# Direction 1 of the doubling levels moved to the array's off-diagonal quadrants, and the output norm's root moved from ScalarE to GpSimd

## The reference, cut to what matters

```python
def step(S, inp):
    r_t, w_t, kk_t, a_t, k_t, v_t = inp
    sa = jnp.einsum('bhvk,bhk->bhv', S, -kk_t)
    S = S * w_t[:, :, None, :] + sa[..., None] * (kk_t * a_t)[:, :, None, :] + v_t[..., None] * k_t[:, :, None, :]
    return S, jnp.einsum('bhvk,bhk->bhv', S, r_t)
...
o = outs[0] + outs[1]
mu = jnp.mean(o, -1, keepdims=True)
var = jnp.mean(jnp.square(o - mu), -1, keepdims=True)
o = ((o - mu) * lax.rsqrt(var + RWKV_GN_EPS)).reshape(B, T, BRANCH_WIDTH) * p['rwkv_gn_g'] + p['rwkv_gn_b']
```

## Time and profile before

| | |
|---|---|
| median of 3 runs | 2651.05 us (2650.5 to 2652.39) |
| the profiled execution | 2649.7 us, its span 2645.4 us |
| PE busy, share of the span | 2505.4 us, 95% |
| DVE busy, share of the span | 1384.3 us, 52% |
| the four passages of layer 2, from the first gram matrices to the tail | about 2041 to 2236 us |
| the same of layer 1 | about 741 to 936 us |

### The profile page before, as it was taken

One profiled execution on the slowest core, in us unless ns is written; L12 is line 12 of the kernel. 1 busy time (PEld: TensorE's weight loads), 2 busy tenths in 40 slices (PEclk: granted clock), 3 DMA queues, 4 the chain that ended last, 5 costly groups with the idle time before them and its releaser, 6 DMA issues.

```text
span 2645.4 us, 56785 instructions
## 1 busy us (share of the span) xinstructions
PE 2505.4 (95%) x23398; PEld 2338.5 (88%) x23398; DVE 1384.3 (52%) x2306; ACT 1053.0 (40%) x1709; POOL 329.2 (12%) x316
## 2 busy tenths in 40 slices
PE   5999999999989999999979999999999999899998
PEld 3888989889988888999968899998898889899997
DVE  2333355576587655443353334646766775644434
ACT  3333244355633434332253332434555342343323
POOL 0000032000033304000100001210001332220001
PEclk7999999999999998999989999999999999989999
DMA  8766634332300023446466665333232000334373
GB/s 271 245 221 191 192 92 135 88 90 81 104 3 4 28 62 97 127 128 203 119 210 220 222 193 157 106 110 86 87 89 72 4 4 27 103 99 126 114 222 108
DMA packets 482186, 319.95 MB, mean 121 GB/s; under 512 B 15474, under 2 KB 438920, under 8 KB 481800
## 3 DMA queue, kind: packets, MB, share of 16 engines
q1 hardware_dynamic: 481928, 316.32, 39.1%
HBM read 311.30 MB, written 4.98 MB: 120 GB/s over the span
## 4 chain that ended last, share of the span: by engine, by line
PE 43%; DVE 4%; issue 1%; ACT 1%; POOL 1%; DMA 0%; SPq 0%; DVEq 0%; ACTq 0%; POOLq 0%
PE acc L849 11%; PE acc L851 10%; PE acc L850 10%; PE pb L1204 3%; PE acc L1204 2%; PE pb L903 1%; PE pb L911 1%; PE pb L918 0%; PE pb L1132 0%; POOL ln_sum L2033 0%; DVE xt L2533 0%; PE pb L1151 0%; PE pb L849 0%; DVE w_lo L2147 0%; PE pb L1119 0%
## 5 line engine op out<-in xcount | busy, mean ns | idle before, releaser
L849 PE MATMUL acc<-xm_hi,w_hi 128*128 128x384 f32 x2352 | 810.5, 345 | 37.3 <-DVE xm_lo L2157 33.1
L851 PE MATMUL acc<-xm_hi,w_lo 128*128 128x384 f32 x2352 | 795.3, 338 | 0.0
L2147 DVE TENSOR_TENSOR w_lo<-raw,w_hi 128x1024 fp32r<-128x1024 f32 (+1 forms) x420 | 521.4, 1241 | 510.8 <-ACT w_hi L1581 502.6
L850 PE MATMUL acc<-xm_lo,w_hi 128*128 128x384 f32 x2320 | 784.3, 338 | 0.0
L1581 ACT ACTIVATE w_hi<-raw 128x1024 fp32r<-128x1024 f32 (+1 forms) x420 | 438.8, 1045 | 284.9 <-PE acc L851 180.1
L849 PEld LDWEIGHTS acc<-xm_hi,w_hi 128*128 128x128 f32 x2352 | 448.6, 191 | 80.1 <-issue 50.8
L851 PEld LDWEIGHTS acc<-xm_hi,w_lo 128*128 128x128 f32 x2352 | 447.8, 190 | 0.0
L850 PEld LDWEIGHTS acc<-xm_lo,w_hi 128*128 128x128 f32 x2320 | 442.3, 191 | 0.5
L849 PE MATMUL acc<-h_hi,w_hi 128*128 128x384 f32 x704 | 242.6, 345 | 8.2 <-DVE w_lo L2147 8.1
L851 PE MATMUL acc<-h_hi,w_lo 128*128 128x384 f32 x704 | 239.9, 341 | 0.0
L850 PE MATMUL acc<-h_lo,w_hi 128*128 128x384 f32 x704 | 239.6, 340 | 0.0
(11 more groups left out here) (364 smaller groups left out, 3476.3 us busy)
## 6 DMA issues: line engine op xcount, KB each, us to landing
raw<-in_ffn_w_in SPq DMA_DIRECT2D x179, 512.0 KB, 4.0
modw<-in_w_mod SPq DMA_DIRECT2D x71, 1024.0 KB, 6.1
raw<-in_w_in SPq DMA_DIRECT2D x114, 512.0 KB, 4.0
raw<-in_ffn_w_out SPq DMA_DIRECT2D x64, 512.0 KB, 4.9
raw<-in_ffn_w_out SPq DMA_DIRECT2D x32, 384.0 KB, 3.6
raw<-in_w_up SPq DMA_DIRECT2D x24, 512.0 KB, 3.5
modx<-in_w_mod SPq DMA_DIRECT2D x9, 1024.0 KB, 12.8
raw<-in_w_out SPq DMA_DIRECT2D x16, 512.0 KB, 4.4
```

The costliest lines, as they stand in the source:

```text
L849: pe.matmul(out, lhs[0], rhs[0], start=first, stop=False)
L850: pe.matmul(out, lhs[0], rhs[1], start=False, stop=False)
L851: return pe.matmul(out, lhs[1], rhs[0], start=False, stop=last)
L2147: done(dve.tensor_tensor(w_lo[:, c % SPL, 0:w], raw[:, c % RAW, 0:w], w_hi[:, c % SPL, 0:w].bitcast(F32), ALU.subtract), lo_done)
```

## The change

Direction 1's products of `ltm` and `xi` and its U go to the off-diagonal quadrants: the matmul that reads partitions 0 to 63 writes PSUM partitions 64 to 127, and the other way round. So that the halves match, `xt` of direction 1 is kept with its heads swapped; the transpose that starts direction 1 is therefore done twice, straight and crossed, and the last level of direction 1 crosses `xt` back, with one more group of multiplications by the identity (DVE then copies instead of adding).

The order on PE changes. lx of direction 0 and U of direction 1 of the level before alternate matmul by matmul in one block of 48 records (`level_lx0_u1`). So do U of direction 0 and lx of direction 1 (`level_u0_lx1`). Each UT stands by itself. Two pairs of PSUM banks change roles from level to level (`lx_bank`, `u_bank`). `prepare_decay` moves one step back.

The output norm's root goes: DVE scales and shifts the variance, POOL raises it to -0.5 (`tensor_tensor` with `pow`, an operation that no instruction before uses), and PE's `tile_root` stands at level 5 behind `tile_gate`, ahead of UT of direction 1. DVE's and ACT's side steps between the level steps are spread anew.

```diff
 
         def early_bank(m):
 return pb[(m + 2) % 4]
+
+        def lx_bank(n, d):
+return pb[d + 2 * (1 - n % 2)]
+
+        def u_bank(n, d):
+return pb[d + 2 * (n % 2)]
 
         def gbank(key):
 if key == ("w", 0) or key == ("w", 1):
...
                 sub_spread_out(units[u - 2])
             if u >= 1:
                 weigh(units[u - 1])
-        def quads(out, lhs, rhs, start, stop):
-
-            for hp in HALVES:
-                mm = pe.matmul(out[hp], lhs[hp], rhs[hp], start=start, stop=stop, skip_group_check=True)
+        def quads(out, lhs, rhs, start, stop, cross=False):
+
+            for i, hp in enumerate(HALVES):
+                mm = pe.matmul(out[HALVES[1 - i] if cross else hp], lhs[hp], rhs[hp], start=start, stop=stop,
+                               skip_group_check=True)
             return mm
 
         def turn_vtok(j):
...
 
         def turn_start(j, d):
 
-            pe.wait_ge(gram_read, 6 * j + 3 + d)
+            pe.wait_ge(gram_read, 6 * j + 3 + 3 * d)
             pe.wait_ge(xt0_ready, 2 * j + d + 1)
             for q in range(NQ):
                 mm = quads(pb[d][:, q * CH:(q + 1) * CH], xts[j % 2][:, NQ * d + q, :], id64, True, True)
+                if d == 1:
+                    mm = quads(pb[3][:, q * CH:(q + 1) * CH], id64, xts[j % 2][:, NQ + q, :], True, True, True)
             mm.then_inc(xi_t, 1)
 
-        def level_lx(j, n, d):
+        def lx_ready(j, n, d):
 
             pe.wait_ge(ltm_ready, 2 * NL * j + 2 * (n - 1) + d + 1)
             pe.wait_ge(xi_ready, 2 * NL * j + 2 * (n - 1) + d + 1)
+
+        def u_ready(j, n, d):
+
+            pe.wait_ge(tl_ready, 2 * NL * j + 2 * (n - 1) + d + 1)
+            pe.wait_ge(xt_ready, 2 * (NL + 1) * j + 2 * (n - 1) + d + 1)
+            if n == 1:
+                pe.wait_ge(gram_read, 6 * j + 5 + d)
+
+        def lx_quads(n, d, q):
+            return quads(lx_bank(n, d)[:, q * CH:(q + 1) * CH], ltm[:, NQ * d + q, :], xi[:, NQ * d + q, :],
+                         True, True, d == 1)
+
+        def u_quads(j, n, d, q):
+            return quads(u_bank(n, d)[:, q * CH:(q + 1) * CH], xts[j % 2][:, NQ * d + q, :], tl[:, NQ * d + q, :],
+                         True, True, d == 1)
+
+        def ut_quads(j, n, d, q):
+
+            out, cross = lx_bank(n, d)[:, q * CH:(q + 1) * CH], n == NL and d == 1
+            if cross:
+                quads(out, id64, xts[j % 2][:, NQ * d + q, :], True, False, True)
+            return quads(out, tl[:, NQ * d + q, :], xts[j % 2][:, NQ * d + q, :], not cross, True, cross)
+
+        def level_lx0_u1(j, n):
+
+            lx_ready(j, n, 0)
             if n > 1:
-                pe.wait_ge(xt_ready, 2 * (NL + 1) * j + 2 * (n - 1) + d + 1)
+                u_ready(j, n - 1, 1)
             for q in range(NQ):
-                mm = quads(pb[d][:, q * CH:(q + 1) * CH], ltm[:, NQ * d + q, :], xi[:, NQ * d + q, :], True, True)
-            mm.then_inc(tl_done, 1)
-
-        def level_xlx(j, n, d):
-
-            pe.wait_ge(tl_ready, 2 * NL * j + 2 * (n - 1) + d + 1)
-            if n == 1:
-                pe.wait_ge(xt_ready, 2 * (NL + 1) * j + d + 1)
-                pe.wait_ge(gram_read, 6 * j + 5 + d)
-            if n < NL:
-                for q in range(NQ):
-                    mm = quads(pb[2 + d][:, q * CH:(q + 1) * CH], xts[j % 2][:, NQ * d + q, :], tl[:, NQ * d + q, :],
-                               True, True)
-                mm.then_inc(u_done, 1)
+                lx = lx_quads(n, 0, q)
+                if n > 1:
+                    uu = u_quads(j, n - 1, 1, q)
+            lx.then_inc(tl_done, 1)
+            if n > 1:
+                uu.then_inc(u_done, 1)
+
+        def level_u0_lx1(j, n):
+
+            u_ready(j, n, 0)
+            lx_ready(j, n, 1)
             for q in range(NQ):
-                mm = quads(pb[d][:, q * CH:(q + 1) * CH], tl[:, NQ * d + q, :], xts[j % 2][:, NQ * d + q, :], True, True)
+                uu = u_quads(j, n, 0, q) if n < NL else ut_quads(j, n, 0, q)
+                lx = lx_quads(n, 1, q)
+            uu.then_inc(u_done if n < NL else ut_done, 1)
+            lx.then_inc(tl_done, 1)
+
+        def level_ut(j, n, d):
+
+            if n == NL:
+                u_ready(j, n, d)
+            for q in range(NQ):
+                mm = ut_quads(j, n, d, q)
             mm.then_inc(ut_done, 1)
 
...
+            level_ut(j, 1, 0)
             if old:
                 turn_new(s)
                 scan_update(s, 3)
             if nxt:
                 prepare_rate(j + 1, 0)
                 prepare_rate(j + 1, 1)
-            level_xlx(j, 1, 1)
             for n in range(2, NL + 1):
-                level_lx(j, n, 0)
-                level_lx(j, n, 1)
+                level_lx0_u1(j, n)
+                level_ut(j, n - 1, 1)
                 if n == 2:
                     if nxt:
                         prepare_norm(j + 1)
                     if old:
                         tile_sums(s)
-                if n == 5:
+                if old and n == 4:
+                    tile_var(s)
+                if n == NL:
                     start_states(j)
-                    if old:
-                        tile_gate(s)
-                level_xlx(j, n, 0)
-                if old and n == 3:
-                    tile_var(s)
-                if old and n == 4:
+                level_u0_lx1(j, n)
+                if old and n == NL:
+                    tile_gate(s)
                     tile_root(s)
-                level_xlx(j, n, 1)
+                level_ut(j, n, 0 if n < NL else 1)
         pieces = iter([(m, k) for m in range(EARLY_PB) for k in (0, 1)] + [(m, 2) for m in range(EARLY_PB)]
                       + [(m, k) for m in range(EARLY_PB, EARLY) for k in (0, 1, 2)])
...
         def tile_square(j):
             act.wait_ge(gn_moved, 2 * j + 1)
             done(act.activation(guc[:, 1, :], osum[:, :], ACT.Square), gn_taken)
-
-        def tile_std(j):
-            act.wait_ge(gn_var, j + 1)
-            done(act.activation(gnr[:, :, :].rearrange("p c h -> p (c h)"), acc[2][:, 0:2 * NCH], ACT.Sqrt, scale=1.0 / HD,
-                                bias=eps[:, 2:3]), gn_taken)
 
         def tile_affine(j):
...
                 link(pool.tensor_tensor(ksum[:, j % 2, :], ksum[:, j % 2, :], kt[:, 1, :], ALU.add))
             done(pool.tensor_tensor(aa[:, d, :], aa[:, d, :], kk[:, :], ALU.mult), key_ready)
 
+        def tile_root(j):
+            pool.wait_ge(gn_scaled, j + 1)
+            flat = gnr[:, :, :].rearrange("p c h -> p (c h)")
+            done(pool.tensor_tensor(flat, flat, root_of[:, 0:1].to_broadcast([128, 2 * NCH]), ALU.pow), gnr_ready)
+
         def tile_low(j):
             pool.wait_ge(brc_hi_s, j + 1)
             done(pool.tensor_tensor(brc_lo[:, j, :], osum[:, :], brc_hi[:, j, :].bitcast(F32), ALU.subtract
...
             for n in range(1, NL + 1):
                 mask(j, n, 0)
                 mask(j, n, 1)
+                if n == NL and old:
+                    tile_root(j - 1)
                 if n == 3 and nxt:
                     rate(2 * j + 2)
                     rate(2 * j + 3)
...
             dve.wait_ge(xi_t, 2 * j + d + 1)
             done(dve.tensor_tensor(xi[:, u, :], pb[d][:, 0:TOK].rearrange("p (q s) -> p q s", q=NQ),
                                    over(id64, NQ), ALU.add), xi_ready)
-            done(dve.tensor_tensor(xts[j % 2][:, u, :], xts[j % 2][:, u, :], over(id64, NQ), ALU.add), xt_ready)
-
-        def level_add(j, n, d):
+            src = xts[j % 2][:, u, :] if d == 0 else pb[3][:, 0:TOK].rearrange("p (q s) -> p q s", q=NQ)
+            done(dve.tensor_tensor(xts[j % 2][:, u, :], src, over(id64, NQ), ALU.add), xt_ready)
+
+        def add_u(j, n, d):
+
+            mine = xi[:, NQ * d:NQ * d + NQ, :].rearrange("p q s -> p (q s)")
+            dve.wait_ge(u_done, 2 * (NL - 1) * j + 2 * (n - 1) + d + 1)
+            done(dve.tensor_tensor(mine, mine, u_bank(n, d)[:, 0:TOK], ALU.add), xi_ready)
+
+        def add_ut(j, n, d):
 
             u = slice(NQ * d, NQ * d + NQ)
-            if n < NL:
-                dve.wait_ge(u_done, 2 * (NL - 1) * j + 2 * (n - 1) + d + 1)
-                mine = xi[:, u, :].rearrange("p q s -> p (q s)")
-                done(dve.tensor_tensor(mine, mine, pb[2 + d][:, 0:TOK], ALU.add), xi_ready)
             dve.wait_ge(ut_done, 2 * NL * j + 2 * (n - 1) + d + 1)
             mine = xts[j % 2][:, u, :].rearrange("p q s -> p (q s)")
-            done(dve.tensor_tensor(mine, mine, pb[d][:, 0:TOK], ALU.add), xt_ready)
+            if n == NL and d == 1:
+                done(dve.tensor_copy(mine, lx_bank(n, d)[:, 0:TOK]), xt_ready)
+            else:
+                done(dve.tensor_tensor(mine, mine, lx_bank(n, d)[:, 0:TOK], ALU.add), xt_ready)
 
         def scaled_states(out, new, by):
 
...
             done(dve.tensor_tensor(guc[:, 0, :], cmix[:, 8 + j, :], acc[3][:, 0:TOK], ALU.mult), bonus_read)
 
         def tile_root(j):
```

(91 more changed lines are left out.)

34 lines of the change are left out of this document (13 added, 21 removed).

## The result

The changed kernel takes 2656.73 us (median of 19 runs) against 2651.89 us for the kernel before in the same series, a ratio of 1.0019 with a 95% interval of 1.0012 to 1.0026. It is about 5 us slower, just inside the 0.2% that I had called no change, and 1.7 us above the top of my range. I had forecast 2630. One of the 19 runs took 6060.2 us; the ratio leaves it out, and without it the median is 2656.65. The profiled execution took 2654.88 us, its span 2653.1.

A forecast was written before the change was run, and what follows sets the result against it. PE was taken to bound passages 1 to 3, with DVE not far behind. Per layer 3.4 + 2 x (2.0 - 1.0) + 5.3 - 0.2 = 10.5 us, 21 in two layers, from 2651 to 2630 us; range 2612 to 2655.

The forecast's parts named there:

- The blocks: Mixed lx and U blocks on PE: 48 records over four quadrants in 0.70 us; the other bound was 1.40.
- D: Rival for PE's blocks: quadrants do not overlap, a block takes 1.40 us, kernel 2667 us; chance 0.15.
- E: Rival for PE's blocks: half an overlap, a block near 1.1 us, kernel 2650 to 2655 us; chance 0.08.
- PE's work and what fills in behind: Each passage's PE list: 28 groups become 20 units, at most 5.6 us less; a bare level takes 3.2 us, waiting 0.4.
- Passage 0: First passage's level stretch: ends 22.2 us after its start against 25.9; 3.4 us less counted.
- The stall at the root: Level 5, passages 1 and 2: PE stands some 3.6 us plus POOL's root p, for DVE's late `tile_root`.
- the clock: Behind the stall in passages 1 and 2, PE runs at half of 2.4 GHz; 1.0 us counted in each.
- The power: POOL's root p: 0.5 us taken, 0.1 to 3 kept as range, counted 8 times; first-use 6 us left out.
- Passage 3: Last passage's level stretch: DVE is free, so the end comes at 22.4 + p against 28.2; 5.3 us less.
- The tail: End of each layer: POOL's power replaces ACT's 0.27 us root; 0.2 us more.
- passages 1 and 2: Middle passages' level stretches: ending at 28.3 to 29.1 plus p, 2.0 us less each, before 1.0 for the clock.
- Rival C: Root on POOL is dear, p of 2.5 to 3 us; kernel 2646 to 2650 us; chance 0.13.

The follow-up runs named there:

- hold_load: Changed kernel with SyncE's three 512 KB up-projection loads in passage 3 held until the passage's last lx group; 2653.21 us, 1.0008 of the kernel before.
- early_root: Changed kernel with DVE's `tile_root` moved up, right behind the add of U of direction 1 at level 4; 2638.21 us, 0.9945 of the kernel before.

## Why the prediction was wrong, step by step

- **The blocks**: right. 48 records in 0.71 us; rivals D and E fell. Against E the working had only that the eight records of L903 start within 1.06 us, and that agrees with a floor of 25 ns just as well. Their single starts in the same trace decide it: four of them come 6 to 7 ns apart.
- **PE's work and what fills in behind**: this is the step that failed. I had a unit at 0.70 us wherever its inputs were ready, and a bare level at 3.2 us with 0.4 us of waiting. Two things were left out. DVE's four adds and its side steps fill the level: 4.48 us in passage 1, so level 5 began 20.4 us into the stretch and not 18.7, and DVE's scaling for the root was done at 27.7 us (passage 2: 26.6) and not at 25.1 to 26.2. I named no price for the side steps of 1.11 and 0.95 us (`prepare_keys`) at these levels; there were no gaps to take them. And PE's instructions come no faster than 256 in 3.5 to 4.0 us, which groups on two quadrants had used up already. Nothing in the earlier trace rows could show that: these groups are short. Passage 0 came out at 23.2 and 24.4 us for 22.2, with 2.3 and 2.0 us of gaps in the middle of groups.
- **The stall at the root**: right, 4.49 us for 3.6 + 0.5, in the place that I named. That the clock would fall behind it was right too, 1.3 us for 1.0. One sum was wrong: scaling at 25.1 to 26.2, root 0.81 and two units 1.40 give an end of 27.3 to 28.4 plus p, not 28.3 to 29.1. At full clock PE took 2.0 us from the gather of the root to the gram matrix. So 0.7 to 1.0 us in each of these four passages stood for nothing, and hid part of the miss. What I did not ask is whether one step of 0.17 us had to stand at the end of DVE's list.
- **The power**: 1.34 us where I took 0.5, eight times 0.84, 6.7 us. The Trainium skill ("GPSIMD Engine Reference", section "Instruction dispatch") gives some 6 us for the first call to newly loaded code; nothing of it is to be seen here. The power lasts 1.32 to 1.34 us each time, the first included, and the wait at the first root is as long as the later ones.
- **Passage 3**: 28.5 us for 22.9 (27.6 in layer 1). The root held PE for 1.54 us, as laid out but for the power's size. The rest is the 2.76 us without instructions, the clock behind it (0.94 over the stretch), and again levels slower than 3.2 us.
- **The tail**: 1.0 us in each layer for 0.2.

Between 2630 and 2656.7 lie 26.7 us. By place, against what I had laid out, both layers together: passage 0 3.2, passages 1 and 2 8.6, passage 3 10.3, the tail 1.6. Another 2.3 lie in the first halves of the passages, which I took as unchanged: in passages 2 and 3 they are 0.6 to 1.0 us longer, in 1 shorter. And 0.8 lie in the kernel before itself, 2651.9 in this series for 2651.05. The places are read from the two profiled executions, whose spans differ by 7.7 us where the medians differ by 4.8, so that they add up so well is in part luck.

By cause it closes less well, and most of these terms are counted, not measured one by one. In passages 1 and 2 the scaling for the root came 2.1 and 0.9 us later than the middle of what I had laid out, in both layers 6.0; the power gives 3.4 (four times 0.84), the clock 1.3 (5.3 measured, 4.0 counted); the wrong sum takes back some 3.4. Of passage 3's 10.3 us the power is 1.7 and the supply beside the loads 3.5 (hold_load). Some 5 us there stay open. So does how much of the blocks' unused gain is due to DVE's list and how much to the supply; no run lightened DVE's list alone.

Rival C had the direction, with a power at 2.5 to 3 us; what was dear was the power's size, the supply and DVE's list together.

## What to carry to other kernels

Before work is put side by side on one engine, ask what feeds that engine: here its instructions came no faster than the old groups had used them, and the next engine's list was as long as the level. When an operation is moved to another queue, look at both ends of its chain; the same power cost 18 us more at the end of DVE's list than nine instructions earlier, and a wait of 4.5 us cost another 1.3 us in clock. A large load that nobody needs yet can still cost time, when it passes beside transfers that somebody does need.

## What the runs showed that I had not expected

- PE took 256 instructions (128 matmul records, 128 weight loads) per transfer of 16 KB, and began no more than one such burst in 3.5 to 4.0 us in a stream without waits. The Trainium skill ("Runtime: NRT & Kernel Launch", section "Instruction fetch mechanics") says that instructions come in blocks of 16 KiB, 256 of them, and that crossing a boundary is mostly hidden. The size agrees (3.11 MB in 190 transfers). That it is hidden holds for the groups of the kernel before, where PE has no such wait at L1204, and not for these blocks.
- Beside three loads of 512 KB at 300 to 390 GB/s two such transfers lay 6.5 us apart; without the loads, 3.7 to 4.0.
- Two groups on different pairs of quadrants, issued one after the other, overlapped by 0.3 of 1.4 us.
- A power of six elements a partition took GpSimd 1.34 us, more than a product of 384 elements (1.00 us). In early_root, where DVE works beside it in passages 1 and 2, it took 1.64 to 1.65 us.
